# Context tiles' attention items between full ones, and half of the attention gate projected last

## The reference

```python
for l in range(2):
    last = l == 1
    parts = split_in(h @ w_in[l])              # h: the normed image tokens
    q = mla_q(parts[0], ...)                   # 8 heads of 96
    k, v = mla_kv(parts[1], parts[2], ...)
    ...                                        # the same for the context tokens: kc, vc
    attn = attend(q, concat([kc, k]), concat([vc, v]))          # 1280 keys
    y_a = attn * silu(g_a)
    y_b = sc_b * dwconv(sc_c * sc_in, sc_conv_w) * silu(g_b)    # 3 taps
    z = dwconv(a * sigmoid(g), cf_conv_w) + cf_conv_b           # 31 taps
    y_c = (silu(layer_norm(z)) @ cf_pw_w + cf_pw_b) * silu(g_c)
    x = x + gate * (concat([y_a, y_b, y_c]) @ w_out[l])
    if not last:
        attn_c = attend(qc, kc, vc)            # context queries see the 256 context keys alone
        ...                                    # mixer and output projection for the context
```

## Time and profile before

| | |
|---|---|
| time, median of 3 runs | 4806.51 us (4799.42 to 4820.97) |
| profiled execution, its own time | 4792.71 us |
| its span, first to last instruction | 4790.9 us |
| mean granted clock of TensorE | 0.932 |
| PE busy | 4214.7 us (88%) |
| DVE, ACT, POOL busy | 1976.7, 1355.2, 520.7 us |
| layer 0: projection's last tiles, attention | to 574 us, 591 to 953 us |
| layer 1: the same | to 1532 us, 1544 to 1865 us |

### The profile page before, as it was taken

One profiled execution on the slowest core, in us unless ns is written; L12 is line 12 of the kernel. 1 busy time (PEld: TensorE's weight loads), 2 busy tenths in 40 slices (PEclk: granted clock), 3 DMA queues, 4 the chain that ended last, 5 costly groups with the idle time before them and its releaser, 6 DMA issues. The chain is left out here.

```text
span 4790.9 us, 69010 instructions
## 1 busy us (share of the span) xinstructions
PE 4214.7 (88%) x28006; PEld 2454.2 (51%) x28006; DVE 1976.7 (41%) x3936; ACT 1355.2 (28%) x3135; POOL 520.7 (11%) x562
## 2 busy tenths in 40 slices
PE   5999899999998999999997745788698799999994
PEld 2455466644444665354556534677585344433431
DVE  1454256611562664322007666666345322222224
ACT  2124445511244553111014454333032111111110
POOL 0000000000000000000010001222001422322220
PEclk8999989999999999999998967998897899999997
DMA  5122330131323203411111030000303578999995
GB/s 190 59 72 63 107 119 18 41 128 41 94 82 115 88 18 138 154 53 60 44 64 40 2 103 2 3 3 3 115 1 144 204 258 282 335 303 336 334 332 156
DMA packets 185014, 563.09 MB, mean 118 GB/s; under 512 B 24577, under 2 KB 95858, under 8 KB 171250
## 3 DMA queue, kind: packets, MB, share of 16 engines
q1 hardware_dynamic: 146402, 433.38, 25.0%
q0 software_dynamic: 38288, 125.19, 9.4%
HBM read 435.71 MB, written 122.80 MB: 117 GB/s over the span
## 5 line engine op out<-in xcount | busy, mean ns | idle before, releaser
L729 PE MATMUL banks<-arena 128*128 128x512 f32 (+1 forms) x2928 | 1125.7, 542 | 15.0 <-DMA arena<-in_w_in 9.3
L729 PEld LDWEIGHTS banks<-arena 128*128 128x128 f32 x2928 | 559.1, 192 | 548.7 <-issue 504.0
L3326 PE MATMUL banks<-arena 128*32 128x512 f32 (+2 forms) x2896 | 560.9, 595 | 4.1 <-DMA arena<-in_experts 3.3
L1240 PE MATMUL banks<-arena 128*128 128x256 f32 (+1 forms) x1152 | 376.3, 481 | 19.3 <-DMA arena<-y_d 14.8
L3326 PEld LDWEIGHTS banks<-arena 128*32 128x32 f32 (+2 forms) x2896 | 198.4, 130 | 357.8 <-issue 354.0
L1446 PE MATMUL banks<-arena 96*128 96x512 f32 (+1 forms) x800 | 331.7, 550 | 42.6 <-DMA arena<-k_d 35.1
L1497 DVE TENSOR_REDUCE arena<-banks 128x1 f32<-128x512 f32 (+1 forms) x400 | 226.5, 593 | 262.9 <-PE banks L1446 262.9
L1240 PEld LDWEIGHTS banks<-arena 128*128 128x128 f32 x1152 | 221.7, 194 | 165.1 <-issue 145.5
L3345 PE MATMUL banks<-arena 128*32 128x512 f32 (+2 forms) x1448 | 286.4, 595 | 1.7 <-DVE arena L3375 1.2
L3410 ACT ACTIVATE arena<-banks 128x256 f32<-128x256 f32 x79 | 30.5, 386 | 781.1 <-PE banks L3326 781.1
L3293 POOL DMA_INDIRECT r_d<-arena x125 | 181.5, 1452 | 639.2 <-DVE arena L3375 509.0
(11 more groups left out here) (502 smaller groups left out, 5693.7 us busy)
## 6 DMA issues: line engine op xcount, KB each, us to landing
arena<-in_experts SPq DMA_DIRECT2D x64, 3072.0 KB, 12.9
arena<-in_ada_w SPq DMA_DIRECT2D x12, 2048.0 KB, 7.8
arena<-in_w_in SPq DMA_DIRECT2D x19, 1024.0 KB, 5.7
arena<-in_w_mod SPq DMA_DIRECT2D x8, 2048.0 KB, 15.9
arena<-in_w_in SPq DMA_DIRECT2D x7, 2048.0 KB, 8.6
arena<-in_w_out SPq DMA_DIRECT2D x6, 2048.0 KB, 11.4
arena<-in_tokens SPq DMA_DIRECT2D x4, 2048.0 KB, 18.2
arena<-in_w_mod SPq DMA_DIRECT2D x8, 1024.0 KB, 5.2
```

Source lines behind the costliest of these rows:

```text
L729: i = e.matmul(self.out_of(n), lhs, rhs, start=k == 0, stop=k == KT - 1)
L1240: i = e.matmul(bank(n % 4)[:, 0:nn], w[:, q, :], H[:, q, t0:t0 + nn], start=q == 0, stop=q == KT - 1)
L3326: op = e.matmul(ABK[(q - q0) % 2][rows, :], xT[(q - q0) % 2][:, P * k:P * k + P][:, rows], weights[:, i % SLOTS, 512 * k:512 * k + 512], s ...
```

## The change

The four parts, in the order of the diff:

- In the projection stage the last 256 of the 512 columns of `ga` become a job of their own, `ga2`, behind `gc`. The weights are now twelve pieces instead of eleven (two of 256 columns in the place of one of 512). The gates' products on DVE start when `gc` is done (`gated_at`), and POOL issues the `y_d` stores ahead of the last two stores of `ga2`.
- In layer 0, too, a row of `preparation` begins every 5/2 steps.
- In the attention of layer 0 the tiles are taken in the order 2, 0, 3, 1, 4 to 9, and tiles 2 and 0 (then 3 and 1) take turns by pairs of heads: two full items, two context items, eight times. `before` finds the item that last used a bank. Queries have a third buffer.
- The values are loaded in two halves (heads 0 to 3, heads 4 to 7), and the queries of the second tile come ahead of the keys of head 1, in both layers.

```diff
-            self.starts = [base + 3 + (5 * n // 2 if last else 3 * n) for n in range(len(self.rows))]
+            self.starts = [base + 3 + 5 * n // 2 for n in range(len(self.rows))]
...
-            self.total = self.into.step(len(self.plan.tiles))
+            self.gated_at = self.into.step(self.plan.ends["gc"] + 1) + 1
...
-            o, n = SEGS["ga"]
-            jobs.append(job("fm", "ga", W, o, o + n, ACT.Silu, blocks=blocks, dst=u1, row0=o))
+            def attention_gate(nm, o):
+                jobs.append(job("fm", nm, W, o, o + 256, ACT.Silu, blocks=blocks, dst=u1, row0=o))
+
+            attention_gate("ga", SEGS["ga"][0])
             for nm, buf, after in (("gb", "sc", "short"), ("gc", "ca", "long")):
                 o, n = SEGS[nm]
                 jobs.append(job("pad", nm, W, o, o + n, ACT.Silu, blocks=blocks, dst=pair(buf), after=after))
+            attention_gate("ga2", SEGS["ga"][0] + 256)
...
-                    (slot + self.total, self.end.gates(dve)), *self.prep.vector_lanes(dve, slot)]
+                    (slot + self.gated_at, self.end.gates(dve)), *self.prep.vector_lanes(dve, slot)]
...
-            self.prep.gpsimd(e), self.into.gpsimd(e), self.end.gpsimd(e)
+            self.prep.gpsimd(e)
+            between = self.plan.place[self.plan.ends["ga2"]] - 1
+            self.into.gpsimd(e, range(0, between))
+            self.end.gpsimd(e)
+            self.into.gpsimd(e, range(between, len(self.plan.stores)))
...
-        QT = [reg(o + 1024 * i, 1024, 96).rearrange("p (h t) -> p h t", h=HN) for i in range(2)]; o += 2048
+        QT = [reg(q, 1024, 96).rearrange("p (h t) -> p h t", h=HN) for q in (o, o + 1024, ST + 2560)]; o += 2048
...
-        items = [(ti, h) for ti in range(ti0, NT) for h in range(HN)]
+        seq = list(range(2, NT)) if last else [2, 0, 3, 1] + list(range(4, NT))
+        turn = {ti: r for r, ti in enumerate(seq)}
+        beside = {} if last else {2: 0, 3: 1}
+        pairs = [(t, hp) for ti in range(2, NT) for hp in range(0, HN, 2) for t in ((ti, beside[ti]) if ti in beside else (ti,))]
+        items = [(ti, hp + i) for ti, hp in pairs for i in range(2)]
...
+        def before(n, q, step=1):
+
+            return next((i for i in range(n - step, -1, -step) if q < len(parts(i))), None)
...
-            queries(0), keys_of(0), keys_of(1)
-            load(V, B["v_d"].rearrange("(j p) n -> p j n", p=P), "v")
-            for h in range(2, HN):
+            queries(0), keys_of(0), queries(1), keys_of(1), values_of(0), keys_of(2), keys_of(3), values_of(1)
+            for h in range(4, HN):
                 keys_of(h)
-            queries(1), gates(0), gates(1)
+            queries(2), gates(0), gates(1)
...
-            for r in range(2, NT - ti0):
-                e.wait_ge(*Tn.at("scores", HN * (r - 1) - 1, parts(HN * (r - 1) - 1)[-1][0]))
-                queries(r)
+            for r in range(2, len(seq)):
+                if r >= 3:
+                    n = final_of[seq[r - 3]]
+                    e.wait_ge(*Tn.at("scores", n, parts(n)[-1][0]))
+                    queries(r)
                 e.wait_ge(*Vn.at("gated", r - 2))
                 gates(r)
...
             def scores(n, q, j0, jn):
                 ti, h = items[n]
-                if n and q < len(parts(n - 1)):
-                    e.wait_ge(*Sn.at("exp", n - 1, q))
+                if before(n, q) is not None:
+                    e.wait_ge(*Sn.at("exp", before(n, q), q))
```

More of the change, by code:

```diff
@@ L760, in scalar, with gpsimd @@
                 yield
-        def gpsimd(self, e):
+        def gpsimd(self, e, part=None):
             S, plan = self.S, self.plan
             Tn, Vn, Sn, Gn = points(S)
-            for q, n in enumerate(plan.stores):
+            for q in part or range(len(plan.stores)):
+                n = plan.stores[q]
                 e.wait_ge(*Sn.at("out", n))
@@ L1392, in attention @@
         rv = [reg(o, 128), reg(o + 128, 128)]; o += 256
-        QT = [reg(o + 1024 * i, 1024, 96).rearrange("p (h t) -> p h t", h=HN) for i in range(2)]; o += 2048
+        QT = [reg(q, 1024, 96).rearrange("p (h t) -> p h t", h=HN) for q in (o, o + 1024, ST + 2560)]; o += 2048
         assert o <= LIM
         gav = u1[416:928, :].rearrange("(k p) t -> p k t", p=P)
-        items = [(ti, h) for ti in range(ti0, NT) for h in range(HN)]
+        seq = list(range(2, NT)) if last else [2, 0, 3, 1] + list(range(4, NT))
[3 more added lines that the diff above has]
+        items = [(ti, hp + i) for ti, hp in pairs for i in range(2)]
         N = len(items)
         keys = lambda n: 2 if items[n][0] < 2 else NT
+        final_of = {ti: max(n for n in range(N) if items[n][0] == ti) for ti in seq}
         parts = lambda n: [(q, j0, min(4, keys(n) - j0)) for q, j0 in enumerate(range(0, keys(n), 4))]
         value = lambda m: bank(6 + m % 2)
+        def before(n, q, step=1):
+            return next((i for i in range(n - step, -1, -step) if q < len(parts(i))), None)
         def halves(m):
@@ L1412, in queries, with values_of @@
             def queries(r):
[L1413 to L1414 removed]
+                row = QK * seq[r]
+                load(QT[r % 3], B["q_d"][row:row + QK, :].rearrange("p (h t) -> p h t", h=HN), "q", r)
             def keys_of(h):
                 load(KTt[:, h, :], B["k_d"][:, T * h:T * h + T], "k", h)
+            def values_of(i):
+                load(V[:, :, 256 * i:256 * i + 256], B["v_d"][:, 256 * i:256 * i + 256].rearrange("(j p) n -> p j n", p=P), "v", i)
             def gates(r):
[L1420 to L1424 removed]
+                load(gab[r % 2], gav[:, :, P * seq[r]:P * seq[r] + P], "ga", r)
+            queries(0), keys_of(0), queries(1), keys_of(1), values_of(0), keys_of(2), keys_of(3), values_of(1)
+            for h in range(4, HN):
                 keys_of(h)
[L1426 removed]
+            queries(2), gates(0), gates(1)
             load(H[:, 4:8, P * ti0:T], y_d[512:1024, P * ti0:T].rearrange("(k p) t -> p k t", p=P), "convolved")
@@ L1439, in scores @@
                 ti, h = items[n]
-                if n and q < len(parts(n - 1)):
-                    e.wait_ge(*Sn.at("exp", n - 1, q))
+                if before(n, q) is not None:
+                    e.wait_ge(*Sn.at("exp", before(n, q), q))
                 if q == 0 and h == 0:
-                    e.wait_ge(*ld.at(S, "q", ti - ti0))
-                if q == 0 and ti == ti0:
+                    e.wait_ge(*ld.at(S, "q", turn[ti]))
+                if q == 0 and ti == seq[0]:
                     e.wait_ge(*ld.at(S, "k", h))
-                op = e.matmul(bank(q)[:, 0:P * jn], QT[(ti - ti0) % 2][:, h, :], KTt[:, h, P * j0:P * (j0 + jn)], start=True, stop=True)
+                op = e.matmul(bank(q)[:, 0:P * jn], QT[turn[ti] % 3][:, h, :], KTt[:, h, P * j0:P * (j0 + jn)], start=True, stop=True)
                 op.then_inc(Tn.hit("scores", n, q), 1)
             def turned(n, q, j0, jn):
-                if n and q < len(parts(n - 1)):
-                    e.wait_ge(*(Vn if q == 1 else Sn).at("turn", n - 1, q))
+                if before(n, q) is not None:
+                    e.wait_ge(*(Vn if q == 1 else Sn).at("turn", before(n, q), q))
                 e.wait_ge(*Sn.at("exp", n, q))
@@ L1458, in products @@
                 b, nk = value(m), keys(2 * m)
-                if m == 0:
-                    e.wait_ge(*ld.at(S, "v"))
+                if items[2 * m][0] == seq[0] and items[2 * m][1] % 4 == 0:
+                    e.wait_ge(*ld.at(S, "v", items[2 * m][1] // 4))
                 if half == 0 and m >= 2:
@@ L1547, in core_scalar @@
                 for q, j0, jn in parts(n):
-                    if n >= 2 and q < len(parts(n - 2)):
-                        e.wait_ge(*Tn.at("turn", n - 2, q))
+                    if before(n, q, 2) is not None:
+                        e.wait_ge(*Tn.at("turn", before(n, q, 2), q))
                     e.activation(pr[n % 2][:, P * j0:P * (j0 + jn)], bank(q)[:, 0:P * jn], ACT.Exp, bias=c[:, 3:4], scale=-1.0, accum_out=c[:, 4 + q:5 + q]).then_inc(Sn.hit("exp", n, q), 1)
```

4 lines of the change are left out of this document (2 added, 2 removed).

## The result

The changed kernel took 4779.5 us (median of nine runs, 4771.42 to 4790.35), the kernel before 4804.48 us: a ratio of 0.9949, interval 0.9934 to 0.9965. So it is faster by 0.51%, just at the bound of what can be told from no change; the forecast was 4792 us, with 4775 to 4811 as its range. The profiled execution took 4771.42 us (span 4769.5 us) against 4792.71 us before. Of these 21.3 us, 19.2 lie ahead of the end of layer 1's attention, which comes at 1845.98 in place of 1865.17.

What follows compares the result with a forecast made beforehand. PE was taken as busy nearly everywhere, standing still or slow at projection's end and in layer 0's attention; 8.1 us (tails) + 6.8 us (attention) = 14.9 us, so 4806.5 - 14.9 = 4792 us, range 4775 to 4811.

Steps and rivals of the forecast that it cites:

- The tail: From projection's last matmul to SP's first attention load: 4.73 us in both layers, gaining 7.36 us and 0.72 us.
- the cover: Projection's end: half gate's PE steps behind `gc`, 34.7 and 27.8 us, under which DVE's products and POOL's stores finish.
- The rows: Layer 0's projection: rows every 5/2 steps clear the end for `ga2` but give nothing by themselves, 0 us.
- The bound of 4 us either way: Layer 0's projection: three segments of `conv_end` could each move by a wait like the 1.33 us one.
- The other bound, 14.6 us lost: Layer 0's projection: all 11 rows beside the long convolution wait for DVE as long as one did, 1.33 us.
- The attention: Layer 0's attention: context items cost 40.64 us before; eight pairs at 4.05 us and 1.4 us of start gain 6.8 us.
- The group: Layer 0's attention: two full and two context items take 13.85 us, including waits of 0.56 and 0.53 us.
- The late query: Attention: tile 1's queries, behind tile 2's gates in SP's loop, cost at most 1 us, once; taken as 0.
- The rival that waits vanish in the mix: Layer 0's attention: context work and full items fill each other's waits, gaining 16.9 us, 4781 us in all; chance 0.17.
- the rival of the falling clock: Layer 0's attention: the switches' waits keep or bring PE to 0.50, 4827 to 4885 us; chance 0.07.
- the 1.4 us of the start: Layer 0's attention: added because its third set of scores begins 14.01 us after the first in place of 8.38 us.
- The loads: Both attentions: values in halves and the second tile's queries ahead of head 1's keys, taken as 0 us.

Runs made afterwards that it cites:

- the gate whole: Changed kernel with the attention gate undivided in its old place and the convolutions' products and stores last again: 4788.66 us, 0.9968 of the kernel before.
- a block: Changed kernel with layer 0's context items not alternating but all together behind full tile 2: 4774.1 us (0.9940 of the kernel before), again 4771.17 us (0.9939).
- the context-first kernel: Changed kernel with layer 0's items in the old order, context tiles 0 and 1 first, nothing alternating: 4788.33 us, 0.9961 of the kernel before.

## Why the prediction was right, and where not

The time came out in the range, 12.5 us below the forecast: the medians differ by 25.0 us, where 14.9 were forecast. To the end of layer 1's attention the profiled executions differ by 19.2 us, where 14.9 were forecast: 3.82 more in layer 0's projection, 0.50 in the tails, 1.09 in layer 1's start, less 0.46 in the attention and some 0.6 in small intervals. The other 5.8 of the 25.0 us lie behind that or between single executions and medians; nothing in the change explains them, so how near the whole time came to the forecast says less than the intervals do. By the prediction's steps:

- **The tail, 7.36 + 0.72 us forecast, 7.85 + 0.73 measured.** The sum was right and the reason only half of it. "If the cover were gone, these 7.4 us would be back" failed: without the half gate behind, 0.73 us come back in layer 0. The denser rows alone bring 12.09 to 4.97 us, the half gate alone to 5.37, both to 4.24. I had read the late stores as late for lack of cover, while DVE's order, products behind the last row, made them late. The extra 0.5 us: POOL's issue to SP's load took 3.31 us in layer 0 (570.50 to 573.81), 3.79 in layer 1 as before. The Trainium skill, "DMA: Bandwidth & Descriptors", section "Anatomy of one DMA — SWDGE (gpsimd) path", whose figures gave an estimate of 2.6 us for the store, stays below both intervals, which also hold the kernel's `gate()`.
- **The rows, 0 forecast, 3.82 us gained.** This is the step that failed: "It gives nothing by itself." The bound of 4 us either way was worked out from waits; what moved was the clock behind waits of nearly the same sum, and that 3.82 lies just inside 4 is luck. The 3.82 us are of two executions, and by the others it could be up to 8.1; with the gate whole it was 0.46. The other bound, 14.6 us lost, was too small for a spacing one half step denser (26.4 us): PE's waits on DVE came to 16.6 us, near the bound, and the clock, which it left out, fell besides.
- **The attention, 6.8 us forecast, 6.34 measured.** The group, 13.85 us forecast, took 13.90, with both waits. The late query, taken at 0 and bounded by 1 us, cost 0.94. The sum held because it was taken from whole intervals of the trace; its reason, "The gain is that the clock rises under the full items", is only a part, since 5.47 of the 40.64 us were a wait for keys, which the prediction did not look for. "The interleaving itself gives little" was still too kind: against a block it costs 3.85 us, about 2.8 for seven more returns and 0.94 for the late query. The rival that waits vanish in the mix gave nearly the time that came out (4781 us), but its mechanism fell, since both waits stand in every group; so did the rival of the falling clock. (The first rival's 16.9 us gained leave out the 1.4 us of the start that the other sums hold; with them it is 15.5 us, and its time 4783 us.) The Trainium skill, "TensorE: Matmul & The Clock Gate", section "Loop structure matters more than you think", calls a loop cold that has a long wait for a DMA between every matmul. The block's waits of 0.35 and 0.56 us are on ACT and DVE, and it ran at 1.00 for some 28 us; the context-first kernel, which has waits of 2.43 and 4.60 us for a DMA among its first items, ran those at 0.50. What differs is what ran before the context items and these longer waits; the two are not told apart here.
- **The loads, 0 forecast.** Right for the values; for the query it holds only because the change moved it ahead. Left where it was, attention took 9.0 us more.
- **Layer 1's start**, 1.1 us better, was mostly spread; nothing was forecast for it.

Open: why the middle segment's wait of 2.08 us left the clock up in eight of nine executions with the denser rows and in none of three with the old ones; how much of what the context items lost in front was the clock and how much followed from the waits for keys; and by how much whole times of single kernels drift behind layer 1's attention.

## What to carry to other kernels

Put short, wait-ridden items behind dense ones rather than between them: the dense work brings the clock up and gives the later heads' loads time to land, the block keeps the clock, and each return to dense items has its price. Where a stage ends late, look first at what the last producer is queued behind on its own engine; here moving that was as good as adding cover, and the two did not add up. A spacing that looked free in one engine's busy share moved the clock of another, in both directions.

## What was not expected of the hardware

Eight matmul instructions of 128x512 took 3.70 us behind a wait of 2.48 us, in nine of nine executions, and 5.12 to 6.77 us behind one of 3.20 us, in three of three; behind 2.08 us both 3.70 and 5.40 us were seen. Context pairs ran at the full clock for some 28 us (624.91 to 653.16), 3.70 us a pair, with two waits of 0.35 and 0.56 us in each, having come to it behind full items, where the kernel before, with nothing dense ahead and a wait for keys among the first items, took 5.47 us for such a pair.
